# A norm summed by columns, its root on four columns and spread by one matmul, and two MLP units sharing the first tiles

## The reference

```python
x = x + rmsnorm_2(merged @ w_out[l], norm_mix_post[l])
h = rmsnorm_2(x, norm_mlp_pre[l])
f = jnp.square(jax.nn.relu(h @ w_ff_in[l])) @ w_ff_out[l]
x = x + rmsnorm_2(f, norm_mlp_post[l])
```

## Time and profile before

| | value |
| --- | --- |
| median of three runs | 2508.78 us |
| the profiled execution | 2509.79 us |
| its span on the engines | 2507.6 us |
| mean granted TensorE clock | 0.978 of full |
| PE busy | 2397.1 us, 96% |
| DVE, ACT, POOL busy | 52%, 32%, 34% |
| bytes moved | 217.5 MB, mean 87 GB/s |

### The profile page before, as it was taken

The page is one execution under the profiler, slowest core; times in us unless marked ns, Lnnn a source line. Parts: engine busy times, 40 slices in busy tenths (PEclk is TensorE's granted clock), DMA queues, the critical chain, the costliest instruction groups (busy, mean ns, idle before and its releaser), DMA issues.

```text
span 2507.6 us, 28122 instructions
## 1 busy us (share of the span) xinstructions
PE 2397.1 (96%) x11057; PEld 1911.8 (76%) x11057; DVE 1298.4 (52%) x1593; ACT 814.1 (32%) x909; POOL 862.1 (34%) x198
## 2 busy tenths in 40 slices
PE   6998999999998999989999999999999996999996
PEld 5888776788886888886667888887887774888884
DVE  6476344454446554664435534486457546631624
ACT  4232334332222332323343322222326523322320
POOL 2322122344443343222224444444323222443440
PEclk9999999999999999999999999999999997999997
DMA  5332133344445443322223444454844232444440
GB/s 123 85 77 58 34 68 68 84 91 93 100 100 118 126 99 87 68 51 47 62 61 85 100 100 94 90 139 114 172 101 82 63 74 52 96 89 101 94 91 34
DMA packets 200167, 217.50 MB, mean 87 GB/s; under 512 B 14456, under 2 KB 181512, under 8 KB 199304
## 3 DMA queue, kind: packets, MB, share of 16 engines
q1 hardware_dynamic: 200072, 216.16, 39.8%
HBM read 206.40 MB, written 9.73 MB: 86 GB/s over the span
## 4 chain that ended last, share of the span: by engine, by line
issue 57%; PE 26%; POOL 13%; DVE 3%; DVEq 1%; ACT 1%; POOLq 0%; ACTq 0%
POOL w_lo L2490 12%; PE psG L345 8%; PE psG L346 8%; PE psG L347 8%; PE psH L2004 1%; PE psH L1989 1%; DVE xT L2471 0%; DVEq L2469 0%; PE psH L2017 0%; PE psH L1957 0%; DVE rms L457 0%; DVE y L2467 0%; PE psH L448 0%; DVE sq L422 0%; POOLq L2487 0%
## 5 line engine op out<-in xcount | busy, mean ns | idle before, releaser
L2490 POOL TENSOR_TENSOR w_lo<-raw,w_hi 128x2048 fp32r<-128x2048 f32 x186 | 860.5, 4627 | 1592.9 <-ACT w_hi L338 1592.9
L345 PE MATMUL psG<-h_hi,w_hi 128*128 128x512 f32 x1640 | 653.8, 399 | 16.4 <-DVE h_lo L466 12.3
L338 ACT CAST w_hi<-raw 128x2048 fp32r<-128x2048 f32 x186 | 354.7, 1907 | 921.5 <-PE psG L347 907.1
L347 PE MATMUL psG<-h_hi,w_lo 128*128 128x512 f32 x1640 | 644.0, 393 | 0.0
L346 PE MATMUL psG<-h_lo,w_hi 128*128 128x512 f32 x1640 | 643.8, 393 | 0.0
L345 PEld LDWEIGHTS psG<-h_hi,w_hi 128*128 128x128 f32 x1640 | 310.6, 189 | 120.9 <-issue 45.3
L347 PEld LDWEIGHTS psG<-h_hi,w_lo 128*128 128x128 f32 x1640 | 310.9, 190 | 66.3
L346 PEld LDWEIGHTS psG<-h_lo,w_hi 128*128 128x128 f32 x1640 | 311.1, 190 | 63.7 <-issue 1.4
L345 PE MATMUL psG<-hid_hi,w_hi 128*128 128x512 f32 x608 | 242.6, 399 | 6.1 <-POOL w_lo L2490 6.1
L346 PE MATMUL psG<-hid_lo,w_hi 128*128 128x512 f32 x608 | 241.0, 396 | 0.0
L347 PE MATMUL psG<-hid_hi,w_lo 128*128 128x512 f32 x608 | 240.9, 396 | 0.0
(11 more groups left out here) (417 smaller groups left out, 3012.8 us busy)
## 6 DMA issues: line engine op xcount, KB each, us to landing
raw<-in_w_in_dram SPq DMA_DIRECT2D x122, 512.0 KB, 6.4
raw<-in_w_gate_dram SPq DMA_DIRECT2D x44, 512.0 KB, 5.9
raw<-in_w_up_dram SPq DMA_DIRECT2D x44, 512.0 KB, 6.3
raw<-in_w_down_dram SPq DMA_DIRECT2D x32, 512.0 KB, 6.3
raw<-in_w_ff_in_dram SPq DMA_DIRECT2D x32, 512.0 KB, 6.2
raw<-in_w_ff_out_dram SPq DMA_DIRECT2D x32, 512.0 KB, 6.2
raw<-in_w_o_dram SPq DMA_DIRECT2D x16, 512.0 KB, 5.6
raw<-in_w_down_dram SPq DMA_DIRECT2D x16, 384.0 KB, 5.4
```

Source lines behind the costliest of these rows:

```text
L338: act.copy(w_hi[:, s, :], raw[:, s, :]).then_inc(hi_done.sem, 1)
L345: pe.matmul(out, a_hi, b_hi, start=first, stop=False)
L347: return pe.matmul(out, a_lo, b_hi, start=False, stop=last)
L2490: pool.tensor_tensor(w_lo[:, s, :], raw[:, s, :], w_hi[:, s, :].bitcast(F32), ALU.subtract)\
```

## The change

The norm behind the output projection:

- ScalarE reads the projection's tiles from PSUM itself, a Square to `sq_y2` and a Copy with the gain to `y2` for each of the eight tiles; VectorE's copies go. ScalarE splits WO+2, WO+3 and FA behind them; VectorE splits FA+1.
- VectorE adds the squares of tiles 0 to 5 up during the projection. Tiles 6 and 7 are not added: TensorE sums the added tile and these two with 12 small matmuls in which the squares are the stationary operand (128x128) and two columns of ones the moving one, accumulating to 128 tokens x 4.
- The root (ScalarE) and the reciprocal (VectorE) work on 128x4. ScalarE multiplies the identity by each of the four columns (`spread`, 128 x 4 x 128), and one matmul with ones sums and spreads that to 128x512 in PSUM.
- VectorE then has per tile a product from `y2` and PSUM into PSUM, an add of it to x, and `h_lo` of the tile before.
- A small Sqrt on one column stands between tiles 6 and 7 on ScalarE.

TensorE's first MLP units: FA and FA+1 share the first four tiles of `h` (12 products for each tile instead of 3), then FA takes tiles 4 to 7, then FA+1. The loop over pairs starts at 1.

The counts of the shared norm semaphores fall by one for the later norms, and the last loop of `post_dve` has one turn less.

```diff
-    sq_y2 = nc.alloc_sbuf_tensor_at("sq_y2", [P, 6, S], F32, offset=h_lo_at)
+    sq_y2 = nc.alloc_sbuf_tensor_at("sq_y2", [P, KD, S], F32, offset=h_lo_at)
+    spread = nc.alloc_sbuf_tensor_at("spread", [P, TB, P], F32, offset=h_hi_at)
...
         for k in range(4):
             pe_feature(pe, *un(V_WO + k), *jn(K_WO + k), m2_hi, m2_lo, merged_tile if k == 0 else None)
-        sum_pe(pe, DEPTH, 2, sq_y2)
+
+        def column_sums(tile, first, last):
+            for c in range(TB):
+                mm = pe.matmul(psH[:, c, 0:2], sq_y2[:, tile, c * P:(c + 1) * P], ones[:, 0:2],
+                               start=first, stop=last)
+            return mm
+
+        pe.wait_ge(y_sum.sem, 1)
+        column_sums(0, True, False)
+        pe.wait_ge(y_sq.sem, 7)
+        column_sums(6, False, False)
+        pe.wait_ge(y_sq.sem, 8)
+        column_sums(7, False, True).then_inc(y_ss.sem, 1)
+        pe.wait_ge(y_dg.sem, 1)
+        pe.matmul(psH[:, 0, :], ones[:, 0:1].broadcast_to([P, P]), spread[:, :, :].rearrange("p t c -> p (t c)"),
+                  start=True, stop=True).then_inc(y_sp.sem, 1)
...
         for half, vf, kf, vd, kd in ((0, V_FA, K_FA, V_DA, K_DA), (1, V_FB, K_FB, V_DB, K_DB)):
-            with pe.Fori(0, 4) as i:
+            if half == 0:
+                pe_first_two(pe, vf, kf, mlp_tile)
+            with pe.Fori(1 - half, 4) as i:
                 for s in range(2):
                     jm, b = step(JB + kf // 2, kf % 2, s)
-                    pe_feature(pe, i + (UB + vf // 2), s, i + jm, b, h_hi, h_lo,
-                               mlp_tile if half == 0 and s == 0 else None)
+                    pe_feature(pe, i + (UB + vf // 2), s, i + jm, b, h_hi, h_lo)
...
+    def pe_first_two(pe, v, j, k_wait):
+
+        for u in range(2):
+            bank_ready(pe, *jn(j + u))
+        for k0, units in ((0, (0, 1)), (4, (0,)), (4, (1,))):
+            for k in range(k0, k0 + 4):
+                if units != (1,):
+                    k_wait(k)
+                for u in units:
+                    m, s = un(v + u)
+                    b = jn(j + u)[1]
+                    if k == 0:
+                        unit_ready(pe, m, s)
+                    wh = w_hi[:, s, :].rearrange("p (k c) -> p k c", k=KD)
+                    wl = w_lo[:, s, :].rearrange("p (k c) -> p k c", k=KD)
+                    for i in range(2):
+                        c = slice(i * P, (i + 1) * P)
+                        mm = triple(pe, psG[:, 2 * b + i, :], wh[:, k, c], wl[:, k, c], h_hi[:, k, :], h_lo[:, k, :],
+                                    k == 0, k == KD - 1)
+                        if k == KD - 1:
+                            mm.then_inc(tick.sem, 1)
...
         for k in range(4):
-            if k:
-                act.wait_ge(y_ok.sem, k)
-                square_pair(act, DEPTH, 1, k - 1, y2, sq_y2)
-            split_next(act, V_WO + k)
-        act.wait_ge(y_ok.sem, 4)
-        square_pair(act, DEPTH, 1, 3, y2, sq_y2)
-        rms_act(act, DEPTH, 2)
+            b = jn(K_WO + k)[1]
+            for j in range(2):
+                n = 2 * k + j
+                act.wait_ge(tick.sem, Tn(V_WO + k, j))
+                act.activation(sq_y2[:, n, :], psG[:, 2 * b + j, :], ACT.Square).then_inc(y_sq.sem, 1)
+                if n == 6:
+                    act.activation(small[:, 62:63], eps_ap, ACT.Sqrt)
+                mm = act.activation(y2[:, n, :], psG[:, 2 * b + j, :], ACT.Copy, scale=par[:, R_POST2 + n:R_POST2 + n + 1])
+            mm.then_inc(psum_free[b].sem, 1)
+            act.drain().then_inc(y_ok.sem, 1)
+            if k < 3:
+                split_next(act, V_WO + k)
+        act.wait_ge(y_ss.sem, 1)
+        act.activation(y_col[:, 0, :], psH[:, :, 0], ACT.Sqrt,
+                       scale=1.0 / D, bias=eps_ap).then_inc(y_sd.sem, 1)
+        act.wait_ge(y_rs.sem, 1)
+        for c in range(TB):
+            mm = act.activation(spread[:, c, :], ident[:, :], ACT.Copy, scale=y_col[:, 1, c:c + 1])
+        mm.then_inc(y_dg.sem, 1)
...
-        for k in range(4):
-            b = jn(K_WO + k)[1]
-            if k >= 2:
-                fold(dve, DEPTH, 1, k - 1, sq_y2)
-            for j in range(2):
-                dve.wait_ge(tick.sem, Tn(V_WO + k, j))
-                mm = dve.tensor_copy(y2[:, 2 * k + j, :], psG[:, 2 * b + j, :])
-            mm.then_inc(psum_free[b].sem, 1)
-            dve.drain().then_inc(y_ok.sem, 1)
-        fold(dve, DEPTH, 1, 3, sq_y2)
-        post_dve(dve, 2, R_POST2, par[:, R_MPRE2:R_MPRE2 + KD])
+        for k in (1, 2):
+            dve.wait_ge(y_sq.sem, 2 * k + 2)
+            tt(sq_y2[:, 0:2, :], sq_y2[:, 0:2, :], sq_y2[:, 2 * k:2 * k + 2, :], ALU.add)
+            dve.drain()
+        tt(sq_y2[:, 0, :], sq_y2[:, 0, :], sq_y2[:, 1, :], ALU.add).then_inc(y_sum.sem, 1)
+        m, s = un(V_FA)
+        dve.wait_ge(lo_done.sem, m * 2 + (s + 1 + lo_done.credit))
+        m, s = un(V_FA + 1)
+        dve.wait_ge(raw_in[s].sem, m * 32 + 32)
+        dve.wait_ge(tick.sem, Tn(V_WO + 3, 1))
+        dve.tensor_copy(w_hi[:, s, :], raw[:, s, :]).then_inc(hi_done.sem, 1)
+        dve.wait_ge(y_sd.sem, 1)
+        dve.reciprocal(y_col[:, 1, :], y_col[:, 0, :]).then_inc(y_rs.sem, 1)
+        dve.wait_ge(y_ok.sem, 4)
+        dve.wait_ge(y_sp.sem, 1)
+        for k in range(KD + 1):
+            if k < KD:
+                tt(psH[:, 1 + k % 2, :], y2[:, k, :], psH[:, 0, :], ALU.mult)
+                dve.drain()
+                tt(xT[:, k, :], xT[:, k, :], psH[:, 1 + k % 2, :], ALU.add).then_inc(x2_ok.sem, 1)
+            if k:
+                gained_lo(dve, DEPTH, KD, k - 1, xT, par[:, R_MPRE2:R_MPRE2 + KD])
```

More of the change, by code:

```diff
@@ L131, in build_in @@
     r_col4 = sb("r_col4", [P, TB])
+    y_col = sb("y_col", [P, 2, TB])
     cur = sb("cur", [P, L_ALL])
@@ L1779, in build_in @@
     y_ok = sem("y_ok")
+    y_sq, y_sum, y_ss, y_sd, y_rs, y_dg, y_sp = (sem("y_sq"), sem("y_sum"), sem("y_ss"), sem("y_sd"), sem("y_rs"),
+                                                 sem("y_dg"), sem("y_sp"))
     x2_ok = sem("x2_ok")
@@ L2034, in second_pe @@
         for half, vf, kf, vd, kd in ((0, V_FA, K_FA, V_DA, K_DA), (1, V_FB, K_FB, V_DB, K_DB)):
-            with pe.Fori(0, 4) as i:
+            if half == 0:
+                pe_first_two(pe, vf, kf, mlp_tile)
+            with pe.Fori(1 - half, 4) as i:
                 for s in range(2):
                     jm, b = step(JB + kf // 2, kf % 2, s)
-                    pe_feature(pe, i + (UB + vf // 2), s, i + jm, b, h_hi, h_lo,
-                               mlp_tile if half == 0 and s == 0 else None)
+                    pe_feature(pe, i + (UB + vf // 2), s, i + jm, b, h_hi, h_lo)
             if half == 0:
-                sum_pe(pe, DEPTH, 3, sq_x2)
+                sum_pe(pe, DEPTH, 2, sq_x2)
             for c in range(4):
@@ L2052, in second_pe @@
                             hidden_tile if c == 0 else None)
-        sum_pe(pe, DEPTH, 4, sq)
+        sum_pe(pe, DEPTH, 3, sq)
         for h in range(2):
@@ L2220, in second_act @@
         for p in range(4):
-            square_pair(act, DEPTH, 2, p, xT, sq_x2)
+            square_pair(act, DEPTH, 1, p, xT, sq_x2)
         for half, vf, kf in ((0, V_FA, K_FA), (1, V_FB, K_FB)):
@@ L2239, in second_act @@
             if half == 0:
-                rms_act(act, DEPTH, 3)
+                rms_act(act, DEPTH, 2)
             for k in range(8):
@@ L2243, in second_act @@
                     act.wait_ge(y_ok.sem, k // 2 + 4)
-                    square_pair(act, DEPTH, 3, k // 2 - 1, y2, sq)
+                    square_pair(act, DEPTH, 2, k // 2 - 1, y2, sq)
                 split_next(act, (V_DA, V_DB)[half] + k)
         act.wait_ge(y_ok.sem, 8)
-        square_pair(act, DEPTH, 3, 3, y2, sq)
-        rms_act(act, DEPTH, 4)
+        square_pair(act, DEPTH, 2, 3, y2, sq)
+        rms_act(act, DEPTH, 3)
     def lg_w(n):
@@ L2410, in second_dve @@
                         .then_inc(m2_lod.sem, 1)
-        for k in range(4):
-            b = jn(K_WO + k)[1]
-            if k >= 2:
-                fold(dve, DEPTH, 1, k - 1, sq_y2)
-            for j in range(2):
-                dve.wait_ge(tick.sem, Tn(V_WO + k, j))
-                mm = dve.tensor_copy(y2[:, 2 * k + j, :], psG[:, 2 * b + j, :])
-            mm.then_inc(psum_free[b].sem, 1)
-            dve.drain().then_inc(y_ok.sem, 1)
-        fold(dve, DEPTH, 1, 3, sq_y2)
-        post_dve(dve, 2, R_POST2, par[:, R_MPRE2:R_MPRE2 + KD])
+        for k in (1, 2):
[20 more added lines that the diff above has]
+                gained_lo(dve, DEPTH, KD, k - 1, xT, par[:, R_MPRE2:R_MPRE2 + KD])
         for p in range(1, 4):
-            fold(dve, DEPTH, 2, p, sq_x2)
+            fold(dve, DEPTH, 1, p, sq_x2)
         for half, vf, kf, vd, kd in ((0, V_FA, K_FA, V_DA, K_DA), (1, V_FB, K_FB, V_DB, K_DB)):
@@ L2438, in second_dve @@
             if half == 0:
-                inverse_rms(dve, DEPTH, 3)
+                inverse_rms(dve, DEPTH, 2)
```

(14 more changed lines are left out.)

## The result

| | before | after |
| --- | --- | --- |
| median of four runs | 2508.86 us | 2484.63 us |
| the profiled execution, its span | 2509.79, 2507.6 us | 2484.56, 2482.4 us |
| ratio after to before | | 0.9906, 95% interval 0.9888 to 0.9923 |

The change makes the kernel 24 us faster. The stretch that the forecast is about came out within 0.2 us of it; the other 10 to 11 us come from stages in which no instruction was changed. So the first thing to see is where in the program the two traces part.

The account below looks back on a forecast made before the run. TensorE, busy 96% of the span, was taken as the bound, so only its standstills or slow places count. FA+1 ending 15.2 us earlier, less a 1.15 us wait, gave 14.0 us: 2494.8 us, range 2491.3 to 2499.3.

Parts of the forecast that it names:

- 24 passes on two columns: After WO's last product: TensorE's 12 column matmuls show as 24 passes at 0.12 us, 2.9 us.
- four Copies of the identity: After the reciprocal: ScalarE's four scaled Copies onto 128x128 at 0.37 us each, 1.5 us.
- spread matmul: After the four Copies: one matmul that spreads, at the low clock, 2.1 us; about 1.05 at the high one.
- product and add: VectorE after the spread: product from PSUM, drain, add from PSUM, 0.69 + 0.1 + 0.69 us.
- wait for FA+2: After FA+1: TensorE waits 1.15 us, as FA+2's weights go into FA's slot and are ready 6.6 us after FA's end.
- rival D: VectorE's tile loop in FA and FA+1 is slower by the write to PSUM: 2498.9 us, chance 0.05.
- A: Before FA, the clock doesn't fall; spread and start 2.25 us cheaper: 2491.5 us, chance 0.08.
- B: After WO, passes on two columns are nearly free, sums done at 2090.4: 2492.8 us, chance 0.06.
- C: After WO, column sums run at the low clock (+2.9), which rises after 5.9 us (+0.7): 2498.4 us, chance 0.11.
- E: Behind the first units, the saving isn't kept since POOL's chain of weights is the bound: 2507 us, chance 0.05.
- F: The clock stays at 0.50 through both units FA and FA+1; slower: 2513.5 us, chance 0.03.
- The rest: Outside the changed stretch: counts of the norms and one drain less in the last loop, 0.1 us at most.

Follow-up runs that it names:

- b1: Changed kernel with the new norm, but FA and FA+1 one after the other as before; 2491.3 us.
- b2: Kernel before, arena unchanged, with only FA and FA+1 sharing the first four tiles; 2504.3 us.
- a2: Changed kernel with y_col behind the arena, so that the arena starts where it did before; 2496.7 us.
- a3: Changed kernel with 64 unused bytes more, arena at byte 119296; 2494.6 us.
- b3: Changed kernel with three shared tiles in place of four; 2485.0 us.
- b4: Changed kernel with ScalarE instead of VectorE splitting FA+1, behind its last two evictions; 2486.4 us.
- d1: Changed kernel with its arena 192 bytes further, at byte 119424; 2478.8 us.
- e1: Changed kernel with its arena at byte 119424 and the weight tiles raw, w_hi and w_lo 128 bytes further on; 2527.8 us.
- e2: Changed kernel with arena at 119424, three shared tiles, and VectorE adding tile 6's squares during the projection (16 passes on two columns); 2477.7 us.
- f1: Changed kernel with h_hi, h_lo, the weights and the arena all at 0 modulo 256 bytes; 2479.3 us.
- a1: Kernel before with an unused tile of 32 bytes, so that the arena starts 32 bytes later; 2501.25 us.
- e3: Kernel before with 224 unused bytes, arena at byte 119424; 2494.8 us.
- a4: Kernel before with 96 unused bytes, arena at byte 119296; 2509.7 us.

## Why the prediction was wrong

The mechanism of the change was right, and its terms, counted from WO's end, came out like this:

| term | predicted | measured in after |
| --- | --- | --- |
| 24 passes on two columns | 2.9 | 2.6 (WO's end to the root's start) |
| root, reciprocal, hand-overs | 0.5 | 0.5 |
| four Copies of the identity | 1.5 | 1.28 |
| spread matmul | 2.1 | 1.8 |
| product and add | 1.5 | 1.5 |
| first add to FA's first product | 2.24 | 2.3 |
| FA and FA+1 | 24.0 | 24.2 |
| wait for FA+2 | 1.15 | 1.45 |
| WO's end to FA+2's first product | 35.9 | 35.7 |

Each of them is a step that the prediction named, with the rows it named: L473 for the passes (they start 0.112 apart, there as here; the prediction's 0.12 is not the quotient of its row, 1.05 / 8 = 0.131, and came near the truth all the same), ScalarE's pitch for the narrow copies (0.32 in place of 0.37), 4.9 us of low clock behind the restart where 4.5 were taken, and splits of FA+2 and FA+3 as worked out, one waiting for FA's end, the other for the hidden tiles' copies (2119.05, straight behind them). The spread matmul was shorter since the clock fell only within it: the granted clock is 1.00 up to 2086, 0.72 from there to 2087 and 0.50 behind. VectorE's product into PSUM, for which no row existed, takes 0.69 like a sum with a PSUM source, so rival D had no ground; nor had A (the clock did fall), B (the passes took 2.6) and C (they ran at the high clock), nor E (what was won is kept to the end, in b1 and b2 too) and F (the clock rose after 4.9 us). One slip changes nothing: the load of FA+1's weights comes out at 2081.2 by its own terms, not 2081.5.

That the sum is met within 0.2 us is partly luck. In a2, with the same norm, the passes took 3.0 us and the spread matmul 2.08, and WO's end to FA's first product took 10.9 in place of 10.3; a3, b3, b4, d1, e1, e2 and f1 have 2.07 or 2.08 for the spread matmul too, which is the price forecast. And with the arena held where it was, a2 took 2496.7 us, inside the predicted range and 13.5 below its own before. So the mechanism that the prediction described is the one that ran.

**The step that failed** is "The rest (counts of the norms, one drain less in the last loop) is 0.1 us at most", and with it that stages whose instructions don't change keep their time. The new tile `y_col` stood in the diff and was counted at nothing. It moves the arena by 32 bytes, and that was worth 11.3 us outside the changed stretch in the two profiles (9.0 in the time of a1, 12.1 between a2 and after). The range was made of bounds for the terms of one stretch, and none of the rivals made a stage outside it faster. With the row in hand the prediction could have seen that there was something to ask: products with the same shape cost 0.2333 in WO and 0.2265 in FA, and both figures stand in its text (11.2 us a unit against 10.87) without a word on why.

The prediction used the Trainium skill at two places. The Trainium skill's floor of some 25 ns from start to start of small matmuls (TensorE: Matmul & The Clock Gate, section on 56 ns) is not what bounds these passes: they start 0.112 us apart, and 24 took 2.6. The ScalarE line of the Trainium skill for tiles in SBUF (VectorE: DVE Perf Modes, section on the TRN2 errata) gives as an estimate 0.293 us for a tile of 128 columns; four took 1.28 us here, 0.32 each. VectorE's split of FA+1 took 1.23 us, and that is why it fits under the column sums. The Trainium skill, VectorE: DVE Perf Modes, "The perf-mode tier table", gives 1227 ns for a copy of 2048 f32 columns within SBUF, and the trace agrees.

## What to carry to other kernels

A change to the allocation can change the time of every matmul that reads a tile behind it: when a new tile goes ahead of others, compare the distance between starts of unchanged matmul streams in both traces before giving the result to the edit, and test the edit with the addresses held still. Here one unused tile of 192 bytes is worth 5.8 us, a bad one costs 49, and the thought-out edit gives 14 to 16. When two units share their first tiles, the unit behind them is late by what the second one no longer covers: choose the number of shared tiles by the time that its weights need.

## What the runs showed of the hardware

The distance in bytes between the stationary and the moving operand of an f32r product (128x128 by 128x512), taken modulo 256, goes with the distance between starts in a dense stream: 0.2267 us at 0 (d1, f1, e3), 0.2289 at 64 (after, a1), 0.2333 at 32 (before, a2), 0.2324 to 0.2330 on average at 128 (a3, a4, e1). Moving both by 128 bytes changes nothing (f1, 2479.3 against 2478.8), moving one of them costs 49 us over some 8800 products (e1). Other distances were not tried, nor was 256 told apart from 512 as the period; what in the chip does it is not known from these runs. The distance isn't all: in b3 and b4, at 64 bytes, the products of WO took the 0.2333 of the worse distances, at the addresses at which they take 0.2289 in after.
